# Issuing each 512-column split product of a projection-bound kernel as two 256-column matmuls

## The reference

```
hn = rmsnorm(x) * ln_g
proj = hn @ ssm_w_in                      # 2048 -> z 4096, conv part 6144, dt 64
xs, B, C = silu(causal_conv4(conv part))  # 8 groups, 8 heads of 64, state 128
y = chunked state-space scan(xs*dt, A*dt, B, C) + D*xs
x1 = rmsnorm(x + rmsnorm(y * silu(z)) @ ssm_w_out)     # 4096 -> 2048

shift, scale, gate = split(silu(c) @ w_ada + b_ada)
h = rms_norm(x1) * (1 + scale) + shift
xr, gr, q, kv, k_rope, ga = split(h @ w_in)            # 2048 -> 4160
y_rnn = RG-LRU(causal_conv4(xr)) * silu(gr)
y_att = 8-head latent attention(q, kv, k_rope) * silu(ga)
out = x1 + gate * (concat(y_rnn, y_att) @ w_out)       # 2048 -> 2048
```

## Time and profile before

| | |
|---|---|
| median of 3 runs | 2124.3 us |
| the profiled execution, first to last instruction | 2124.2 us |
| mean granted TensorE clock | 0.998 of full speed |
| MATMUL records, LDWEIGHTS records | 10099, 10099 |
| PE busy, PEld busy | 2113.2 us (99%), 1691.1 us (80%) |
| VectorE busy, ScalarE busy | 1295.7 us (61%), 808.0 us (38%) |

### The profile page before, as it was taken

How to read it: one execution, slowest core, us unless ns; L and a number is a source line. 1 busy time by engine, 2 the same in 40 slices (tenths; PEclk the granted TensorE clock), 3 DMA queues, 4 the chain that set the end, 5 groups by cost and what they waited for, 6 DMA issues and landing times.

```text
span 2124.2 us, 27942 instructions
## 1 busy us (share of the span) xinstructions
PE 2113.2 (99%) x10099; PEld 1691.1 (80%) x10099; DVE 1295.7 (61%) x2147; ACT 808.0 (38%) x1091; POOL 88.1 (4%) x130
## 2 busy tenths in 40 slices
PE   9999999999999999999999999999999999999999
PEld 7888888888888888888878888888887778876887
DVE  5567867777786777777863223263227788667333
ACT  5233433333343333334542222163225456665110
POOL 0000000000000000000000000000000001110000
PEclk9999999999999999999999999999999999999999
DMA  7555655555564555555564343343332232212332
GB/s 221 169 159 152 180 152 165 160 162 164 157 183 145 164 167 168 163 158 165 186 229 158 100 138 129 122 142 116 90 98 82 72 105 79 69 60 71 129 118 99
DMA packets 213873, 294.45 MB, mean 139 GB/s; under 512 B 16098, under 2 KB 150130, under 8 KB 212658
## 3 DMA queue, kind: packets, MB, share of 16 engines
q1 hardware_dynamic: 200738, 256.12, 39.1%
q0 software_dynamic: 8624, 29.04, 5.0%
q10 hardware_dynamic: 4448, 8.45, 1.1%
HBM read 273.51 MB, written 20.05 MB: 138 GB/s over the span
## 4 chain that ended last, share of the span: by engine, by line
PE 97%; DVE 2%; DMA 1%; ACT 0%; issue 0%; SPq 0%; DVEq 0%; ACTq 0%
PE ps L2397 29%; PE ps L2398 29%; PE ps L2399 29%; PE ps L2498 3%; PE ps L2752 1%; PE ps L2777 1%; PE ps L2480 1%; DMA xt<-in_x_dram 1%; PE ps L2756 1%; PE ps L2768 0%; PE ps L2664 0%; PE ps L2482 0%; PE ps L2576 0%; PE ps L2407 0%; PE ps L2612 0%; PE ps L2404 0%
## 5 line engine op out<-in xcount | busy, mean ns | idle before, releaser
L2397 PE MATMUL ps<-hn_hi,w_hi 128*128 128x512 f32 x1264 | 502.7, 398 | 0.0
L2398 PE MATMUL ps<-hn_lo,w_hi 128*128 128x512 f32 x1264 | 499.3, 395 | 0.0
L2399 PE MATMUL ps<-hn_hi,w_lo 128*128 128x512 f32 x1264 | 499.3, 395 | 0.0
L1761 DVE TENSOR_TENSOR w_lo<-w_raw,w_hi 128x1024 fp32r<-128x1024 f32 x174 | 213.0, 1226 | 414.4 <-ACT w_hi L1101 413.2
L1101 ACT ACTIVATE w_hi<-w_raw 128x1024 fp32r<-128x1024 f32 x174 | 183.2, 1057 | 453.1 <-PE ps L2399 414.3
L1499 DVE TENSOR_TENSOR w_lo<-w_raw,w_hi 128x1024 fp32r<-128x1024 f32 x162 | 198.2, 1223 | 211.4 <-ACT w_hi L964 210.9
L964 ACT ACTIVATE w_hi<-w_raw 128x1024 fp32r<-128x1024 f32 x162 | 171.0, 1056 | 409.2 <-PE ps L2399 393.2
L2399 PEld LDWEIGHTS ps<-hn_hi,w_lo 128*128 128x128 f32 x1264 | 236.9, 187 | 57.9
L2397 PEld LDWEIGHTS ps<-hn_hi,w_hi 128*128 128x128 f32 x1264 | 237.1, 188 | 57.5 <-issue 1.2
L2398 PEld LDWEIGHTS ps<-hn_lo,w_hi 128*128 128x128 f32 x1264 | 237.1, 188 | 56.1
L2397 PE MATMUL ps<-w_hi,y_hi 128*128 128x512 f32 x512 | 203.8, 398 | 0.2 <-DVE y_lo L1770 0.2
(11 more groups left out here) (401 smaller groups left out, 2778.2 us busy)
## 6 DMA issues: line engine op xcount, KB each, us to landing
ada_raw<-in_w_ada_dram SPq DMA_DIRECT2D x128, 384.0 KB, 3.4
w_raw<-in_ssm_w_in_dram SPq DMA_DIRECT2D x96, 512.0 KB, 4.6
w_raw<-in_ssm_w_in_dram SPq DMA_DIRECT2D x128, 256.0 KB, 4.2
w_raw<-in_w_in_dram SPq DMA_DIRECT2D x64, 512.0 KB, 3.8
w_raw<-in_ssm_w_out_dram SPq DMA_DIRECT2D x60, 512.0 KB, 3.9
csb<-cs_rows POOLq DMA_DIRECT2D x32, 512.0 KB, 7.2
w_raw<-in_w_out_dram SPq DMA_DIRECT2D x32, 512.0 KB, 4.1
y_rows<-yt POOLq DMA_DIRECT2D x8, 1024.0 KB, 4.7
```

The lines of the kernel that those rows point to most:

```text
L1761: nc.vector.tensor_tensor(w_lo[:, slot, :], w_raw[:, slot, :], w_hi[:, slot, :].bitcast(F32), ALU.subtract).then_inc(lo_ready, 1)
L2397: nc.tensor.matmul(out_, a_hi, b_hi, start=start, stop=False)
L2398: nc.tensor.matmul(out_, a_hi, b_lo, start=False, stop=False)
L2399: return nc.tensor.matmul(out_, a_lo, b_hi, start=False, stop=stop)
```

## The change

A new helper, `product`, stands between `three`, `three_hi_first` and `nc.tensor.matmul`. An output narrower than 512 columns passes through as one matmul, as before. An output of 512 columns is issued as two matmuls with the same stationary operand: moving columns 0 to 255 into the first half of the bank, then columns 256 to 511 into the second. Only the first half carries `start=True`; a semaphore that was attached to the product hangs on the second half.

```diff
+HALF = SEQ // 2
...
+            def product(out_, a, b, start, stop):
+
+                if out_.shape[-1] < SEQ:
+                    return nc.tensor.matmul(out_, a, b, start=start, stop=stop)
+                for h in range(2):
+                    at = slice(h * HALF, (h + 1) * HALF)
+                    mm = nc.tensor.matmul(out_[:, at], a, b[:, at], start=start and h == 0, stop=stop,
+                                          skip_group_check=True)
+                return mm
+
             def three(out_, a_hi, a_lo, b_hi, b_lo, start, stop):
-                nc.tensor.matmul(out_, a_hi, b_hi, start=start, stop=False)
-                nc.tensor.matmul(out_, a_hi, b_lo, start=False, stop=False)
-                return nc.tensor.matmul(out_, a_lo, b_hi, start=False, stop=stop)
+                product(out_, a_hi, b_hi, start, False)
+                product(out_, a_hi, b_lo, False, False)
+                return product(out_, a_lo, b_hi, False, stop)
...
-                nc.tensor.matmul(out_, w_hi_, a_hi, start=start, stop=False)
-                nc.tensor.matmul(out_, w_lo_, a_hi, start=False, stop=False)
+                product(out_, w_hi_, a_hi, start, False)
+                product(out_, w_lo_, a_hi, False, False)
                 pe.wait_ge(lo_sem, count)
-                return nc.tensor.matmul(out_, w_hi_, a_lo, start=False, stop=stop)
+                return product(out_, w_hi_, a_lo, False, stop)
```

## The result

The changed kernel takes 2161.93 us (median of four runs, 2159.27 to 2164.07) against 2124.33 us before. The ratio on record is 1.0168, 95% interval 1.0156 to 1.0180, that is about 36 us more (33 to 38) where 19 us less was forecast.

What follows compares the result with a forecast made beforehand. TensorE's instruction stream was taken to bound the kernel. Halves of 115.5 ns make each of 7944 products 2.4 ns shorter, 19 us less: 2124.2 - 19 = 2105 us, range 2058 to 2190 us.

Steps and rivals of the forecast that it cites:

- What bounds the kernel: Whole span: TensorE's instruction stream, busy 99%, sets the 2124.2 us; ScalarE waits 414.3 us for it in the output projection.
- How many products, and that the second load is issued: Split 512-column products: 7944 of 10099 MATMUL records, adding 7944 matmuls and 7944 really issued weight loads.
- The load's floor: Weight load behind each half: needs 108 to 112 ns, so it just fits in a step of 115 ns.
- The rival in which the load sets a half's step at 118 to 121 ns: Load path full in split products: about 2170 us; chance 0.25, shared with a small fixed cost.
- The column term: Streaming 256 columns in each half: 115.5 ns, a product 2.4 ns less, 19 us less over 7944 products.
- c = -4 ns: Step part not growing with columns, extrapolated from 384- and 512-column matmuls: no positive fixed cost to be seen.
- The upper bound of 126.7: Half's step in ns if the whole 20 ns excess were fixed: 159 us more, 2283 us; chance of c near 20: 0.09.
- I take the step as a property of the matmul, not of the stage: Whole 512-column products: the 233.4 ns step measured in the output projections was taken to hold in every stage.
- Nothing else on TensorE moves: Rest of TensorE's stream: no further change beside the split products' steps; ScalarE's 414.3 us of waiting cover any semaphore shift.
- The clock: TensorE's clock: a level below 1.00 outside the short stretches would be something none of the cases holds.
- The fixed cost per matmul: Each extra matmul: by the skill's fixed 2.5 ns, +20 us; counted with the load path, rows 6 and 9 against.
- Serial loads: Rival for split products: each load has its 188 ns record to itself, 376 ns per product, 3260 us; chance 0.04.

## Why the prediction was wrong

- **What bounds the kernel**: right. TensorE's stream is still the span, and ScalarE waits for it on line 1102 for 421.3 us.
- **How many products, and that the second load is issued**: right, 18043 records.
- **The load's floor**: right, 108 to 112 ns forecast, 111.8 measured beside a stream. The rival in which the load sets a half's step at 118 to 121 ns came nearest to the total (2170 us), for the wrong reason, and that the range of 2058 to 2190 us holds the measured 2162 is luck: its upper part was there for that rival, and 22 of the 37 us come from terms that it doesn't have.
- **The column term**: mis-sized. It said 115.5 ns for a half and 2.4 ns less per product. Measured are 116.6 to 118.4, between 0 and 3.4 ns more per product, 13.4 us in all where -19 was forecast. The failing step is c = -4 ns from the 384-column rows: with halves at 116.67 ns and wholes at 233.33 in the best stage the rate is simply proportional, and 384 columns, still 174 ns in the changed kernel, lie a nanosecond below proportion for a reason of their own. A line through two points, where one is off by a nanosecond, was extrapolated as far again as they lie apart. Of the 56 us between the forecast of 2105 us and the profiled 2161.1, this step makes 32 and the term missing in the next point 22. The upper bound of 126.7 held. The sentence "I take the step as a property of the matmul, not of the stage" failed too: it is so for whole products and not for halves.
- **"Nothing else on TensorE moves"**: wrong, and the sum lacked a whole term, 14.3 us of gaps and 7.8 us of half clock, most of it behind them. I counted the instructions that the engine executes and not those that must be fetched. The page of the kernel before had the line:

```profile
q8 instruction: 39, 0.64, 0.1%
```

  Where the code runs straight on, in the first output projection, six of these 16 KB packets go with 1546 recorded loads and matmuls, some 258 each. At that rate 20198 records would take about 78 packets, so 39 say that the loops ran from memory. It grew to 134 packets.
- **The clock**: I named a lower clock as something no case holds. It came behind five of the six gaps.
- **The fixed cost per matmul**: the 2.5 ns that the Trainium skill gives ("TensorE: Matmul & The Clock Gate", "Back-to-back issue gap") aren't seen where halves take 116.7 ns, half of a whole product's 233.3; its total of 216 ns at 512 columns is not this kernel's either.
- **Serial loads**: fell as forecast. The Trainium skill, "Perfetto Trace Analysis", section "Identifying the Most-Contended Engine", takes the LDWEIGHTS share as one of two measures of headroom; here it rose from 80% to 97% while the time rose by 1.7%. The load records of 0.19 us overlap one another at steps of 0.117 us, so the share tells little of headroom here.

## What to carry to other kernels

Before multiplying the instructions of a hardware loop, look at the instruction queue: if it is silent after the first pass the body still fits, and past that size each back branch takes 3.7 to 5.3 us here, covered only by the time that the queued instructions take. Splitting a matmul can't gain where its step is already proportional to its columns, and a 128-column load puts a floor of 112 ns under every piece at the upper clock. What a gap costs is its length and, behind most gaps of 1.8 us or more here, a stretch at half clock; behind those of 1.1 us or less in the kernel with the first four panels split none came.

## What the hardware showed that I had not expected

- A loop body of 1683 recorded TensorE instructions a pass fits and one of 1875 doesn't; the back branch jumps from 0.2 us to between 3.7 and 5.3 us, ends 1.3 to 1.6 us after an instruction packet has landed, and 16 KB packets run in every pass (60 packets, 0.98 MB, between 280 and 1000 us).
- The clock fell to half and stayed there for 187 us under back-to-back 128-column matmuls without an idle record; at 256 columns a half, in the same stage, it came back after 6.8 us.
- The step of a 256-column half changes when the streamed and the loaded tensor are exchanged (116.5 to 116.9 against 118.3 ns), and can be 116.7 or 117.8 ns with the same tensors, while whole 512-column products take 233.3 ns in every stage.
